# Later adaLN rows in one decoder layer: fp32 matmuls from the loaded weights, in four column groups

## The reference, cut to what matters

```python
mod = jax.nn.silu(c) @ w_ada + b_ada              # c: 9 rows (1 prompt, 8 sample) x 1024; w_ada: 1024 x 6144
sh1, sc1, g1, sh2, sc2, g2 = jnp.split(mod, 6, axis=-1)
h = rmsnorm(x, norm_pre1) * (1 + sc1[:, None]) + sh1[:, None]
proj = h @ w_in                                   # 1024 -> 9232 columns
bg, cg, ua, q, k, v, r, lr, ga, gb = jnp.split(proj, split_idx, axis=-1)
conv_out, conv_buf_new = causal_dwconv(cg * ua, conv_buf, conv_w, conv_b)
y_a = bg * conv_out
# branch B: gated linear attention of 4 heads from q, k, v and the decay, normed, times silu(r)
merged = jax.nn.sigmoid(ga) * y_a + jax.nn.sigmoid(gb) * y_b
x = x + g1[:, None] * rmsnorm(merged @ w_out, norm_post1)
h2 = rmsnorm(x, norm_pre2) * (1 + sc2[:, None]) + sh2[:, None]
a, gt = jnp.split(h2 @ w_up, 2, axis=-1)
f = (jax.nn.gelu(causal_dwconv(a)) * gt) @ w_down
x = x + g2[:, None] * rmsnorm(f, norm_post2)
```

## Time and profile before

| | |
|---|---|
| timed runs, median (lowest to highest) | 1132.45 us (1131.53 to 1133.04) |
| the profiled execution | 1126.76 us |
| its span, first to last instruction | 1125.0 us |
| mean granted TensorE clock | 0.987 |
| busy: TensorE, its weight loads, DVE, ACT, POOL | 96%, 86%, 46%, 36%, 41% |
| moved by DMA | 115.07 MB, 102 GB/s over the span |

### The profile page before, as it was taken

The page is one execution under the profiler, slowest core; times in us unless marked ns, Lnnn a source line. Parts: engine busy times, 40 slices in busy tenths (PEclk is TensorE's granted clock), DMA queues, the critical chain, the costliest instruction groups (busy, mean ns, idle before and its releaser), DMA issues.

```text
span 1125.0 us, 17227 instructions
## 1 busy us (share of the span) xinstructions
PE 1079.3 (96%) x6961; PEld 965.3 (86%) x6961; DVE 516.1 (46%) x681; ACT 409.9 (36%) x588; POOL 458.4 (41%) x206
## 2 busy tenths in 40 slices
PE   3779999999999999899999999999999999999998
PEld 2449878999999999789988887999999999888886
DVE  4541000646677777434423747655445544400204
ACT  6532423333444444333334334433333333211312
POOL 2113243637767667533315302443334333334330
PEclk9879999999999999999999999999999999999999
DMA  9528644898767863686743501233223322222212
GB/s 352 102 41 103 141 112 75 91 103 149 129 121 128 125 132 39 100 66 144 134 113 104 196 1 57 76 94 93 75 80 88 93 75 84 84 75 75 92 66 84
DMA packets 137479, 115.07 MB, mean 102 GB/s; under 512 B 4777, under 2 KB 117185, under 8 KB 136401
## 3 DMA queue, kind: packets, MB, share of 16 engines
q1 hardware_dynamic: 137329, 114.25, 47.7%
q10 hardware_dynamic: 96, 0.04, 0.0%
HBM read 106.92 MB, written 7.35 MB: 102 GB/s over the span
## 4 chain that ended last, share of the span: by engine, by line
PE 72%; issue 16%; POOL 7%; DVE 2%; ACT 1%; DMA 1%; POOLq 0%; DVEq 0%; ACTq 0%
PE pair L1412 43%; PE pair L1452 11%; PE pair L1696 5%; POOL w_lo L694 3%; POOL w_lo L686 3%; PE pair L1497 2%; PE pair L1360 2%; PE pair L1603 1%; PE pair L1591 1%; DMA raw<-in_w_in 1%; PE pair L1564 1%; PE pair L1658 1%; PE pair L1575 1%; PE pair L1615 1%; DVE o_tok L1230 0%
## 5 line engine op out<-in xcount | busy, mean ns | idle before, releaser
L686 POOL TENSOR_TENSOR w_lo<-raw,w_hi 128x1024 fp32r<-128x1024 f32 x102 | 253.5, 2488 | 513.4 <-ACT w_hi L743 513.3
L1412 PE MATMUL pair<-h_hi,w_hi 128*128 128x288 f32 x1600 | 351.2, 298 | 6.9 <-DVE h_lo L1054 6.0
L1412 PE MATMUL pair<-h_hi,w_lo 128*128 128x288 f32 x1600 | 345.7, 294 | 0.0
L1412 PE MATMUL pair<-h_lo,w_hi 128*128 128x288 f32 x1600 | 345.6, 294 | 0.0
L1412 PEld LDWEIGHTS pair<-h_hi,w_hi 128*128 128x128 f32 x1600 | 259.8, 188 | 23.8 <-issue 7.5
L1412 PEld LDWEIGHTS pair<-h_lo,w_hi 128*128 128x128 f32 x1600 | 258.5, 189 | 0.0
L1412 PEld LDWEIGHTS pair<-h_hi,w_lo 128*128 128x128 f32 x1600 | 258.4, 188 | 0.0
L743 ACT ACTIVATE w_hi<-raw 128x1024 fp32r<-128x1024 f32 x118 | 123.7, 1056 | 174.2 <-PE pair L1446 91.5
L694 POOL TENSOR_TENSOR w_lo<-raw_c,w_hi 128x1024 fp32r<-128x1024 f32 x48 | 125.4, 2629 | 55.3 <-ACT w_hi L743 55.3
L743 ACT ACTIVATE w_hi<-raw_c 128x1024 fp32r<-128x1024 f32 x48 | 50.7, 1057 | 93.2 <-PE pair L1412 67.3
L398 DVE SCALAR_TENSOR_TENSOR cv<-ext,ffp,cv 128x592 f32<-128x592 f32 x44 | 82.0, 1863 | 5.7 <-DVE cv L395 3.0
(11 more groups left out here) (268 smaller groups left out, 1347.7 us busy)
## 6 DMA issues: line engine op xcount, KB each, us to landing
raw<-in_w_up SPq DMA_DIRECT2D x44, 512.0 KB, 3.7
raw<-in_w_in SPq DMA_DIRECT2D x40, 512.0 KB, 8.3
raw_c<-in_w_in SPq DMA_DIRECT2D x24, 512.0 KB, 9.4
raw_c<-in_w_ada SPq DMA_DIRECT2D x24, 512.0 KB, 8.2
raw<-in_w_down SPq DMA_DIRECT2D x22, 512.0 KB, 3.5
ada_first<-in_w_ada SPq DMA_DIRECT2D x8, 1024.0 KB, 13.5
raw<-in_w_ada SPq DMA_DIRECT2D x8, 512.0 KB, 5.1
s_in<-in_state_gla SPq DMA_DIRECT2D x8, 512.0 KB, 5.6
```

The lines of the kernel that those rows point to most:

```text
L686: pool.tensor_tensor(lo, raw[r % 2][:, :], hi.bitcast(F32), ALU.subtract).then_inc(S("w_lo_done"), 1)
L1412: ins = pe.matmul(bank[pair][:, half, 0:HALF], w[:, i, :], x[:, i, HALF * half:HALF * half + HALF], start=i == 0 and p == 0, stop=i == KT ...
```

## The change

The rows of `mod` after the first 2048 columns no longer pass through the split. SP loads a `w_ada` tile into one of four buffers of its own (`ada_raw`, which are `raw_c` 0, 1, 4 and 5), and TensorE reads it there as fp32. `c_wide` is silu(c) in fp32, 9 columns padded with zeros to 32. `ada_pair` issues four fp32 matmuls of 32 x 512, one for each of four 128-row blocks, each into another group of 32 partitions of bank 6, that is, with another group of 32 columns of TensorE. Two pairs sum up 512 columns of `mod` in four separate partial sums; DVE copies all 128 partitions, and `mod_back` adds the four with `fold_all` (128 x 9). In a column j the pairs stand behind places 3 and 7.

C1 has 32 tiles in the ring in place of 64. Its channel tiles, and now those of C2, go through four raw buffers in turn (`raw0`, `raw1`, `raw_c2`, `raw_c3`), so that a buffer is loaded again three tiles after its last and not one; the output projection's tile 1 lies over `raw_c2` and `raw_c3` and waits for their last use. The semaphores of the reciprocals are joined into one, and an unused tile of ones is dropped.

```diff
-TILE_C2 = TILE_C1 + 8 * KT
+TILE_C2 = TILE_C1 + 4 * KT
@@ buffers
-    rows_ada = place("rows_ada", [18, 512], offset=g_at + 88064)
+    rows_ada = place("rows_ada", [P, 512], offset=g_at + 88064)
+    c_wide = place("c_wide", [P, KT, 32])
+    fold_sum = place("fold_sum", [P, 64], offset=g_at + 66560)
+    fold_all = place("fold_all", [P, 9])
-    ones = place("ones", [P, P])
+    ada_raw = [raw_c[i] for i in (0, 1, 4, 5)]
     def raw_tile(n):
-        if TILE_C1 <= n < TILE_C2 and n % 8 > 1:
-            return raw_c[n % 8 - 2]
+        if TILE_C1 <= n < TILE_WO and n % 4 > 1:
+            return raw_c[n % 4]
         return raw[n % 2]
     def raw_free(n):
-        if n < 2 or TILE_C1 + 2 <= n < TILE_C1 + 8:
+        if n < 2 or TILE_C1 + 2 <= n < TILE_C1 + 4:
             return 0
-        return n - 7 if TILE_C1 + 8 <= n < TILE_C2 + 2 else n - 1
+        return n - 3 if TILE_C1 + 4 <= n < TILE_WO + 2 else n - 1
@@ SP
+            def load_ada(x):
+                if x >= 4:
+                    sp.wait_ge(S("ada_mm"), (x - 4) // 2 + 1)
+                c0 = 2 * D + 512 * (x // 4)
+                sp.dma_start(k2(ada_raw[x % 4]), ada_v[x % 4, :, :, c0:c0 + 512]).then_inc(S(f"ada_raw_in{x % 4}"), 16)
-            for n in (TILE_C1, TILE_C1 + 1, *range(TILE_C1 + 8, TILE_C2)):
+            for n in (TILE_C1, TILE_C1 + 1):
                 load_c1(n)
+            for i in range(4, 4 * KT):
+                load_c1(TILE_C1 + i)
+                if i >= 6 and i % 2 == 0:
+                    load_ada(i - 2)
+                    load_ada(i - 1)
+            load_ada(4 * KT - 2)
+            load_ada(4 * KT - 1)
@@ ACT, column j of C1
-                n = TILE_C1 + 8 * j
+                n = TILE_C1 + 4 * j
                 high(n + 3)
 ...
-                for m in range(n + 4, n + 8):
-                    high(m)
+                high(n + 4)
+                high(n + 5)
 ...
-                high(n + 8)
-                high(n + 9)
                 if j < KT - 1:
-                    high(n + 10)
+                    high(n + 6)
@@ DVE
+            dve.memset(c_wide[:, :, 9:32], 0.0).then_inc(S("c_split"), 1)
+            dve.tensor_copy(c_wide[:, :, 0:9], c_view).then_inc(S("c_split"), 1)
+            dve.tensor_tensor(fold_sum[:, :], ident[:, 0:64], ident[:, 64:P], ALU.add).then_inc(S("c_split"), 1)
+            dve.wait_ge(S("c_split"), 7)
+            dve.tensor_tensor(fold_all[:, :], fold_sum[:, 0:9], fold_sum[:, 32:41], ALU.add).then_inc(S("c_split"), 1)
-                dve.tensor_copy(rows_ada[:, :], one_bank(6)[0:18, :]).then_inc(S("rows_ada"), 1)
+                dve.tensor_copy(rows_ada[:, :], one_bank(6)[:, :]).then_inc(S("rows_ada"), 1)
@@ TensorE
+            def ada_pair(p):
+                for x in range(2 * p, 2 * p + 2):
+                    pe.wait_ge(S(f"ada_raw_in{x % 4}"), 16 * (x // 4 + 1))
+                if p % 2 == 0 and p > 0:
+                    pe.wait_ge(S("rows_ada"), p // 2)
+                for x in range(2 * p, 2 * p + 2):
+                    for i in range(2):
+                        rows = slice(32 * (x % 2 * 2 + i), 32 * (x % 2 * 2 + i) + 32)
+                        ins = pe.matmul(one_bank(6)[rows, :], c_wide[:, x % 4 * 2 + i, :], k2(ada_raw[x % 4])[:, i, :],
+                                        start=p % 2 == 0, stop=p % 2 == 1)
+                ins.then_inc(S("ada_mm"), 1)
-                    else:
-                        for i in range(2):
-                            ins = ada(one_bank(6)[0:18, :], e // 2 * 2 + i, k2(w_hi[n % 4])[:, i, :], k2(w_lo[n % 4])[:, i, :],
-                                      e == 1 and i == 0, e == 7 and i == 1)
-                        ins.then_inc(S("ring_free"), 1)
+                    elif e % 4 == 3:
+                        ada_pair(2 * j + e // 4)
```

More of the change, by code:

```diff
@@ L76 @@
 LAST = (4, 0, 1, 2, 3)
+RSTD_O = 5
+RSTD_X1 = RSTD_O + 2 * HEADS
+RSTD_F = RSTD_X1 + 2 * TT
 WO_SLOT = [None, None, 0, 1, 2, None, None, 3]
@@ L174, in layer_program @@
     c_sig = place("c_sig", [P, 72], offset=t_at + 8448)
-    c_hl = place("c_hl", [P, KT, 18], F32R)
+    c_hl = place("c_hl", [P, KT, 18], F32R, offset=g_at + 65536)
+    c_wide = place("c_wide", [P, KT, 32])
     fold = place("fold", [18, 9])
+    fold_sum = place("fold_sum", [P, 64], offset=g_at + 66560)
+    fold_all = place("fold_all", [P, 9])
     mix0 = place("mix0", [P, 16, KT])
@@ L681, in _, with low @@
                                pattern=[[TS, NS]], channel_multiplier=-1).then_inc(S("consts"), 1)
-            def low(r, hi, lo, done):
+            def low(n, hi, lo, done):
                 pool.wait_ge(S("w_hi_done"), done)
-                pool.tensor_tensor(lo, raw[r % 2][:, :], hi.bitcast(F32), ALU.subtract).then_inc(S("w_lo_done"), 1)
+                pool.tensor_tensor(lo, raw_tile(n)[:, :], hi.bitcast(F32), ALU.subtract).then_inc(S("w_lo_done"), 1)
             with pool.Fori(0, TILE_C1 // 4) as g:
@@ L690, in _ @@
                     low(r, w_hi[r][:, :], w_lo[r][:, :], g * 4 + (r + 1))
[L691 to L695, removed]
+            with pool.Fori(TILE_C1 // 4, TILE_C2 // 4) as g:
+                for r in range(4):
+                    low(TILE_C1 + r, w_hi[r][:, :], w_lo[r][:, :], g * 4 + (r + 1))
             for r in range(4):
-                low(r, w_hi[r][:, :], w_lo[r][:, :], TILE_C2 + r + 1)
+                low(TILE_C2 + r, w_hi[r][:, :], w_lo[r][:, :], TILE_C2 + r + 1)
             pool.wait_ge(S("decayed"), 2)
             pool.memset(q_own[:, :], 0.0).then_inc(S("p_set"), 1)
-            pool.wait_ge(S("p_set"), 7)
+            pool.wait_ge(S("p_set"), 6)
             pool.wait_ge(S("back"), KT)
@@ L714, in _ @@
                     hi, lo = w_pair(n)
-                    low(r, hi[:, :], lo[:, :], n + 1)
+                    if n == TILE_WO + 1:
+                        pool.wait_ge(S("w_lo_done"), TILE_WO)
+                    low(n, hi[:, :], lo[:, :], n + 1)
             with pool.Fori(TILE_UP // 4, TILES // 4) as g:
                 for r in range(4):
-                    low(r, w_hi[r][:, :], w_lo[r][:, :], g * 4 + (r + 1))
+                    low(TILE_UP + r, w_hi[r][:, :], w_lo[r][:, :], g * 4 + (r + 1))
             for n in range(TILES // 4 * 4, TILES):
@@ L1507, in mod_back @@
                 for m in range(4):
-                    ins = pe.matmul(one_bank(7)[:, 9 * m:9 * m + 9], rows_ada[:, P * m:P * m + P], fold[:, :],
+                    ins = pe.matmul(one_bank(7)[:, 9 * m:9 * m + 9], rows_ada[:, P * m:P * m + P], fold_all[:, :],
                                     start=True, stop=True)
                 ins.then_inc(S("back"), 1)
+            def ada_pair(p):
[9 more added lines that the diff above has]
+                ins.then_inc(S("ada_mm"), 1)
+            pe.wait_ge(S("c_split"), 8)
             for j in range(KT):
                 for e in range(8):
-                    n = TILE_C1 + 8 * j + e
-                    pe.wait_ge(S("w_lo_done"), n + 1)
                     if e % 2 == 0:
+                        n = TILE_C1 + 4 * j + e // 2
+                        pe.wait_ge(S("w_lo_done"), n + 1)
                         before = 4 * j + e // 2 - 3
```

62 lines of the change are left out of this document (29 added, 33 removed).

## The result

The changed kernel takes 1118.24 us (median of 4, 1116.39 to 1119.92) against 1132.36 us (1131.53 to 1133.04), ratio 0.9872 [0.9859, 0.9886]. Its profiled execution took 1116.39 us, with a span of 1114.6.

The account below looks back on a forecast made before the run. The prediction took TensorE, busy for 96% of the span, as the bound. Its terms, -31.0 + 37.9 - 7.0 - 0.8 = -0.9 us, took the timed 1132.45 us to 1131.5 us, range 1108 to 1146.

Parts of the forecast that it names:

- The range: Whole kernel: 1108 to 1146 us, from all four column groups side by side to late loads, leaving out no overlap.
- the likeliest value: Whole kernel: 1131.5 us, with the fp32 matmuls of a pair overlapping as in the staircase.
- the side-by-side rival: `ada_pair` on TensorE: all four column groups run together, 1.06 us a pair, 1110.6 us in all; chance 0.27.
- the staircase: `ada_pair` on TensorE: program order lets each step hide one instruction of the next group, 2.37 us a pair; chance 0.40.
- The bound: Whole kernel: TensorE, busy 96% of the span; time counts if it is TensorE's or TensorE stands still for it.
- Taken away, 31.0 us: 32 `ada` tiles' 128 fp32r matmuls on TensorE's path, 30.4 us, plus 0.6 us where a successor waited for DVE.
- the seam, -7.0 us: C2's first head: earlier loads through `raw_c2` and `raw_c3` end TensorE's wait for `k_tok` and its half clock, -7.0 us.
- Added, 37.9 us: 16 `ada_pair` of four fp32 matmuls on TensorE, 2.37 us each by the staircase, 37.9 us in all.
- `mod_back`: `mod_back` keeps its eight weight loads' time; only the narrow form's gap may go, 8 x -0.1 = -0.8 us.
- SP's order, "I take nothing": Channel-tile loads queued behind `w_ada` loads in C1 still arrive in time, with 4 us to spare: no cost.
- The rival without overlap: `ada_pair` on TensorE: column groups run one after another, 3.67 us a pair, +19.9 us, 1152.3 us; chance 0.12.
- What would show it: Signs in the profile: pairs of 2.37 us, columns of 34.6 us, C2's first head 8.65 us; wrong if pairs take under 2.

Follow-up runs that it names:

- the two profiles taken again: Both kernels profiled and timed again without edits: kernel before 1132.78 us, changed kernel 1116.82 us, ratio 0.9861.
- its seam part alone: Kernel before, with only C2's weight tiles loaded through four raw buffers instead of two: 1126.42 us, ratio 0.9947.

## Why the prediction was right and wrong

At equal pace the 16.7 us are, from one place to the next in the two profiles taken again: +0.6 to the start of the score items; -0.3 in C1's first two columns; -10.0 in the rest of C1; -7.0 at the seam; 0.0 from there to the transposes of `tail_ff`.

- **The range** held, the mechanism that the likeliest value stood on did not. The range had been drawn down to the side-by-side rival; that the time lies in it says nothing for the staircase.
- **The bound** was right: TensorE is 96% busy before and after, and POOL's time off the path was worth nothing.
- **Taken away, 31.0 us, and the seam, -7.0 us**: the sizes were right (8.64 us measured for 8.65 foreseen). The cause of the seam was half the truth. C2's loads through raw_c2 and raw_c3 remove it, but so does taking adaLN tiles out of the ring, which the prediction didn't follow up to the seam; with that alone it is gone too.
- **Added, 37.9 us: this step failed.** "All matmuls of the trace start in program order. If that holds between column groups..." It doesn't. Each group works through its own two passes beside the others, 1.00 us and 0.22 at entry and exit, so 19.5 us in all and not 37.9. The rows held only matmuls on one group (the earlier trace rows too, whose narrow matmuls ran at full pitch one after another); the order that they showed was that group's. Of the two readings of the Trainium skill's "TensorE: Matmul & The Clock Gate", Part 3 (Packing small matmuls), its example of tiles side by side was borne out (starts 6 to 7 ns apart here, 4 ns there), and its sentence that matmuls start in program order was not: with the groups in the order 0, 0, 1, 1 a later one began at least 0.44 us before an earlier one.
- **`mod_back`**: 0.19 us less each, foreseen 0.1.
- **SP's order, "I take nothing"**: the slack was not there. Five loads came late for ACT, three for C1 and the first two of C2, by 1.9 to 7.8 us, 22.3 us together (the waits shown above). TensorE didn't notice, as the prediction had it for that case. But the bunched loads kept an instruction fetch back and cost 3.0 us once. It is the mixed order's price, at a place where I hadn't looked: the prediction asked who waits for the weights, not what else goes through the same queues.
- **The sum with the measured price**: 19.5 - 31.0 - 7.0 - 1.5 + 3.0 + 0.6 = -16.4 us, against -16.7 at equal pace and -14.1 in the first timed medians (-15.5 in the second). What the 0.6 us ahead of the scores are stays open.
- **The rival without overlap** would have been right in its price with one group: 3.55 us a pair for its 3.67, and 1149 us in the one execution, at the quicker pace.
- **What would show it** was well chosen: "wrong if the pairs take less than 2 us", and a column of 32.0 us for side by side, measured 32.24.

## What to carry to other kernels

A small fp32 product with few weight columns is best laid over all four column groups of TensorE: its price was here the passes of the fullest group, whatever the order, and 0.22 us for entry and exit. The raw operand also saves two splits on other engines and slots in the ring. When tiles leave a ring, the rest of the ring reaches further ahead, and a stall far behind may go by that alone. Loads that are issued in bunches can hold back what no wait names, TensorE's instructions among it; spacing the one load that mattered took the stop away (3.3 us between the medians), spacing all cost over 10.

## What the runs showed of the hardware

- Passes of fp32 matmuls (32 weight columns, 512 wide) on one column group follow each other every 0.43 us; those of other groups start 6 to 14 ns apart beside them, also past one that waits.
- In all eight profiles with two weight loads issued 0.5 us apart ahead of it, a fetch of 16 KB of instructions came 31 to 35 us after the one before, and TensorE stood still (0.35 us with one group, 1.2 and 2.4 with two, 2.7 to 3.7 in the others) until 1.2 to 1.4 us after its end. Where the fetch at this place came after 18 to 27 us (the kernel before, also with its seam part alone, and the three with a wait at the loads), TensorE didn't stop.
- Behind the stop the granted clock was 1.00 over the next 5 us in four of these profiles (stops of 0.35, 1.18, 2.99 and 3.05 us) and 0.50 to 0.67 in the other four (2.42, 2.73, 3.35 and 3.69 us), so at its lower level of 0.5 for most of that time. The longer stop didn't always bring the lower clock.
- The 512-byte packets of some loads of `w_in` took 176 to 215 ns on average over 5 us in the changed kernel (225 to 245 us) and 106 to 197 in the kernel before (215 to 260 us), with the queues full, against 28 to 85 and 38 to 116 ns from 260 to 430 us. The changed kernel shows some 165 ns again from 450 to 465 us. Why these loads is open.
- The same program runs its long matmul loop at 130 ns or at 133.3 ns a matmul, from one execution to the next, at the same granted clock of 1.00; what decides it is open, and no run here could set it.
